# One decoder layer in float32 on one core: warm-up matmuls, an earlier first weight block, and first projection units that wait block by block

## The reference

```python
h = rmsnorm(x, attn_norm)
proj = h @ w_in            # columns: q, k, v of group A, q of group B, k and v of group B
out_a = dilated_attention(qa, ka, va, slopes_a)      # 16 heads
out_b = swa_sink_attention(qb, kb, vb, slopes_b, sinks)  # 16 query heads, 2 kv heads
mix = concat(rmsnorm(out_a, out_norm_a), rmsnorm(out_b, out_norm_b))
x = x + mix @ w_out
h = rmsnorm(x, ffn_norm)
x = x + (silu(h @ w_gate) * (h @ w_up)) @ w_down
return rmsnorm(x, final_norm)
```

## Time and profile before

| | |
|---|---|
| median of three runs | 2116.3 us |
| the profiled execution, device time | 2115.78 us |
| its span in the trace | 2114.0 us |
| TensorE matmul busy | 2055.0 us (97%) |
| VectorE busy | 1450.1 us (69%) |
| ScalarE busy | 874.0 us (41%) |
| DMA, mean over the span | 124 GB/s |
| mean granted TensorE clock | 0.992 of full speed |

### The profile page before, as it was taken

The page is one execution under the profiler, slowest core; times in us unless marked ns, Lnnn a source line. Parts: engine busy times, 40 slices in busy tenths (PEclk is TensorE's granted clock), DMA queues, the critical chain, the costliest instruction groups (busy, mean ns, idle before and its releaser), DMA issues.

```text
span 2114.0 us, 35232 instructions
## 1 busy us (share of the span) xinstructions
PE 2055.0 (97%) x12886; PEld 1857.5 (88%) x12886; DVE 1450.1 (69%) x2175; ACT 874.0 (41%) x1380; POOL 119.4 (6%) x191
## 2 busy tenths in 40 slices
PE   8999999999999799999999999999997999999998
PEld 7888888887888699999999999999996888888887
DVE  5466666666665788787887878788785645555446
ACT  5355555554346433333333333333333333333333
POOL 0022222222100000000000000000000000000000
PEclk9999999999999899999999999999998999999999
DMA  6322222224233244344444444344446552534323
GB/s 184 90 73 72 74 75 75 70 74 150 84 112 129 85 141 134 122 137 124 130 129 131 130 121 140 121 130 135 126 130 234 204 175 99 174 123 150 135 99 129
DMA packets 315867, 261.62 MB, mean 124 GB/s; under 512 B 13872, under 2 KB 268128, under 8 KB 314720
## 3 DMA queue, kind: packets, MB, share of 16 engines
q1 hardware_dynamic: 308304, 248.11, 36.9%
q10 hardware_dynamic: 7440, 11.72, 1.6%
HBM read 228.31 MB, written 31.46 MB: 123 GB/s over the span
## 4 chain that ended last, share of the span: by engine, by line
PE 84%; issue 5%; DVE 5%; ACT 4%; DMA 1%; SPq 1%; ACTq 0%; DVEq 0%; POOLq 0%; POOL 0%
PE bank L426 18%; PE bank L428 18%; PE bank L427 18%; PE bank L467 9%; PE bank L468 9%; PE bank L469 9%; PE bank L554 1%; ACT probs L819 1%; ACT w_hi L776 1%; DMA raw<-in_w_down 1%; DVE w_lo L1164 1%; PE bank L571 1%; PE bank L570 1%; ACT qB_both L797 0%; DVE pt_lo L1173 0%
## 5 line engine op out<-in xcount | busy, mean ns | idle before, releaser
L426 PE MATMUL bank<-s_hi,t_hi 128*128 128x256 f32 x2464 | 700.5, 284 | 26.0 <-DVE t_lo L1445 14.7
L427 PE MATMUL bank<-s_lo,t_hi 128*128 128x256 f32 x2464 | 699.2, 284 | 0.0
L428 PE MATMUL bank<-s_hi,t_lo 128*128 128x256 f32 x2464 | 699.2, 284 | 0.0
L1164 DVE TENSOR_TENSOR w_lo<-raw,w_hi 128x512 fp32r<-128x512 f32 x364 | 253.0, 697 | 408.4 <-ACT w_hi L776 406.2
L996 ACT ACTIVATE t_hi<-t_raw 128x1792 fp32r<-128x1792 f32 x176 | 299.6, 1703 | 556.7 <-PE bank L428 539.7
L426 PEld LDWEIGHTS bank<-s_hi,t_hi 128*128 128x128 f32 x2464 | 475.2, 193 | 27.5 <-issue 26.6
L427 PEld LDWEIGHTS bank<-s_lo,t_hi 128*128 128x128 f32 x2464 | 475.1, 193 | 1.0 <-issue 1.0
L428 PEld LDWEIGHTS bank<-s_hi,t_lo 128*128 128x128 f32 x2464 | 475.0, 193 | 0.0
L1445 DVE TENSOR_TENSOR t_lo<-t_raw,t_hi 128x1792 fp32r<-128x1792 f32 x176 | 356.2, 2024 | 155.9 <-ACT t_hi L996 155.9
L776 ACT ACTIVATE w_hi<-raw 128x512 fp32r<-128x512 f32 x364 | 229.1, 631 | 514.3 <-PE bank L469 360.1
L467 PE MATMUL bank<-w_hi,down_hi 128*128 128x512 f32 x640 | 250.1, 391 | 14.3 <-DVE down_lo L1173 14.3
(11 more groups left out here) (162 smaller groups left out, 2283.2 us busy)
## 6 DMA issues: line engine op xcount, KB each, us to landing
raw<-in_w_down SPq DMA_DIRECT2D x176, 256.0 KB, 2.5
t_raw<-in_w_gate SPq DMA_DIRECT2D x174, 256.0 KB, 3.0
t_raw<-in_w_up SPq DMA_DIRECT2D x174, 256.0 KB, 3.4
raw<-in_w_in SPq DMA_DIRECT2D x136, 256.0 KB, 2.9
gu_mid<-gu_out SPq DMA_DIRECT2D x44, 512.0 KB, 3.8
gu_s<-gu_mid SPq DMA_DIRECT2D x44, 512.0 KB, 4.9
raw<-in_w_out SPq DMA_DIRECT2D x64, 256.0 KB, 2.5
x_first<-in_x SPq DMA_DIRECT2D x8, 512.0 KB, 7.7
```

Of the source, the lines that this page charges most:

```text
L426: nc.tensor.matmul(out_ap, st_hi, mv_hi, start=start, stop=False, skip_group_check=True)
L427: nc.tensor.matmul(out_ap, st_hi, mv_lo, start=False, stop=False, skip_group_check=True)
L428: return nc.tensor.matmul(out_ap, st_lo, mv_hi, start=False, stop=stop, skip_group_check=True)
L1164: nc.vector.tensor_tensor(w_lo[:, s, :], raw[:, s, :], w_hi[:, s, :].bitcast(F32), ALU.subtract).then_inc(w_lo_done, 1)
```

## The change

- SP loads w0 right behind x0 rather than behind x1, w1 behind x2, w2 behind x4, w3 behind x6. Each weight block is ahead of one x block that it stood behind.
- TensorE runs eight 128x128 float32 matmuls of `ones` against `ones` into bank 6, which nobody reads, before it waits for the identity and x0.
- The first four units become `first_unit(j)`: the wait for h_lo stands in front of each k, not in front of four, and the two turns of the next x block (`turn_two`) stand in the middle (after the second k) and at the end of units 0 to 2. Before unit 0 only k=0 to 3 are turned.
- ScalarE runs one tiny activation behind the wait for `ones`, which brings its table load forward.
- ScalarE and VectorE split w0 behind k=0 instead of behind k=3.

```diff
--- before.py
+++ after.py
@@ -25,6 +25,7 @@
 NC = D // SEQ
 PAIRS = HEADS // 2
 RING = 4
+WARM = 8
 AHEAD = RING - 1
 UNIT = 512
 WINDOW = 128
@@ -59,7 +60,7 @@
 BANK_X = (2, 3, 5, 7)
 BANK_SET = (BANK_G, BANK_X)
 
-START_SPLITS = ([(0, 0), (0, 1)], [(0, 2)], [(0, 3), (1, 0)], [(1, 1)])
+START_SPLITS = ([(0, 1)], [(0, 2)], [(0, 3), (1, 0)], [(1, 1)])
 FIRST_SQ = 4 * (NC - 1)
 
 LAST = [(t, n) for n in range(NC) for t in (0, 1)] + [(t, n) for t in (2, 3) for n in range(NC)]
@@ -318,7 +319,7 @@
         for n in range(2 * NC):
             cols = slice(256 * n, 256 * (n + 1))
             sp.dma_start(x_first[:, :, cols], x2[:, cols].rearrange("(t p) c -> p t c", p=P)).then_inc(x_loaded[n], 16)
-            if n % 2:
+            if n % 2 == 0:
                 load(0, n // 2, tall(w_in2, n // 2, 4 * D_A), first=True)
         for j in range(4):
             load(1, j, tall(w_in2, j, 4 * D_A + D_KV))
@@ -669,27 +670,37 @@
                         n = KD + 2 * PAIRS
                         nc.tensor.transpose(bank[BANK_PT][:, 0:n], gain_rows[0:n, P:2 * P], ident[0:n, 0:n]).then_inc(gains_turned, 1)
 
+        def turn_two(k0):
+
+            pe.wait_ge(x_loaded[k0 // 2], 16)
+            for k in (k0, k0 + 1):
+                turn_x(k)
+
+        def first_unit(j):
+
+            pe.wait_ge(w_lo_done, j + 1)
+            for k in range(4 * j, 4 * j + 4):
+                pe.wait_ge(xt_lo_done, k + 1)
+                ws = slice(P * (k % 4), P * (k % 4 + 1))
+                mm = three(bank[BANK_Q][:, :], w_hi[:, j, ws], w_lo[:, j, ws], h_hi[:, k, :], h_lo[:, k, :], k == 0, k == KD - 1)
+                if j < 3 and k % 2:
+                    turn_two(k + 3)
+            mm.then_inc(w_used, 1)
+
+        pe.wait_ge(ones_done, 1)
+        for i in range(WARM):
+            nc.tensor.matmul(bank[6][:, 0:P], ones[:, :], ones[:, :], start=True, stop=True)
         pe.wait_ge(ident_loaded, 16)
-
-        for k in range(8):
-            if k % 2 == 0:
-                pe.wait_ge(x_loaded[k // 2], 16)
-            turn_x(k)
-            if k == 1:
-
-                pe.wait_ge(gains_loaded, 16)
-                nc.tensor.transpose(bank[BANK_Q][:, 0:KD], gain_rows[0:KD, 0:P],
-                                    ident[0:KD, 0:KD]).then_inc(gains_turned, 1)
+        turn_two(0)
+        pe.wait_ge(gains_loaded, 16)
+        nc.tensor.transpose(bank[BANK_Q][:, 0:KD], gain_rows[0:KD, 0:P],
+                            ident[0:KD, 0:KD]).then_inc(gains_turned, 1)
+        turn_two(2)
         pe.wait_ge(gains_done, 1)
-        for s in range(8):
-            if s < 4:
-                pe.wait_ge(xt_lo_done, 4 * s + 4)
-            tall_unit(s // 4, s % 4, (BANK_Q, BANK_K)[s // 4], h_hi, h_lo)
-            if s < 2:
-                for k in range(8 + 4 * s, 12 + 4 * s):
-                    if k % 2 == 0:
-                        pe.wait_ge(x_loaded[k // 2], 16)
-                    turn_x(k)
+        for s in range(4):
+            first_unit(s)
+        for s in range(4, 8):
+            tall_unit(1, s % 4, BANK_K, h_hi, h_lo)
             if s == 6:
                 pe.wait_ge(xt_lo_done, KD)
                 spread_r(squares[:, :].rearrange("p (t c) -> p t c", c=P), 1, BANK_PT)
@@ -925,10 +936,14 @@
 
         act.dma_start(gain_rows[0:KD, 0:P], attn_norm[0, :].rearrange("(k p) -> k p", p=P)).then_inc(gains_loaded, 16)
 
+        act.wait_ge(ones_done, 1)
+        nc.scalar.activation(tick[:, 18:19], ones[:, 0:1], ACT.Copy)
         act.wait_ge(gains_done, 1)
         for n in range(NC):
             for k in range(4 * n, 4 * n + 4):
                 x_high(k)
+                if k == 0:
+                    split(0, 0, wait_slot=False)
             for u4, slot in START_SPLITS[n]:
                 split(u4, slot, wait_slot=u4 > 0)
             act.wait_ge(x_loaded[2 * n], 16)
@@ -1351,6 +1366,8 @@
         for n in range(NC):
             for k in range(4 * n, 4 * n + 4):
                 x_low(k)
+                if k == 0:
+                    split(0, 0)
             for u4, slot in START_SPLITS[n]:
                 split(u4, slot)
         for t in range(NT):
```

## The result

| | before | after |
|---|---|---|
| median of six runs | 2116.29 us | 2137.30 us |
| the profiled execution, device time | 2115.78 us | 2139.95 us |
| its span | 2114.0 us | 2138.2 us |
| mean granted TensorE clock | 0.992 | 0.983 |

The ratio is 1.0102, 95% interval 1.0088 to 1.0116. That is within 2%, but it is a real loss of 21 us, clear of the noise, and 20 us above the upper end of the predicted range (2117.2). The forecast was a gain of 1.5 us. One of the six runs before (7181 us) is an outlier; a median is not moved by it.

The account below looks back on a forecast made before the run. TensorE bounds the kernel; ScalarE's chain, set by w2's landing, decides when it enters the loops. The 1.5 us gain gave 2115.78 - 1.5 = 2114.3, or 2114.8 us against the median; range 2113.8 to 2117.2.

Parts of the forecast that it names:

- The step that failed: Whole kernel: the change acts only on the first 40 us, 2% of the span, so 42 us is out of reach.
- The warm-up's price: TensorE's start: eight matmuls end at 4.5 us, before x0 at 5.0; cost nothing, cover 0.5 us.
- Rival 2: TensorE's start: the clock falls in a new pause, losing 2.4 us, to 2117.2 us; chance 10%.
- The order of loads: Loads at the start: w2 lands at 15.1 instead of 16.67, so ScalarE's chain can start 1.55 us sooner.
- TensorE's stretch from x1 to k=7: TensorE's start: at fast pace `x_high` 7 is done at 15.2, a tie with w2's landing; gain 1.5 us.
- rival 1: TensorE from x1 on: clock at 1.2 GHz, 0.6 us slower than before, 2116.9 us; chance 25%.
- the landing of w2: ScalarE's start: w2's arrival, at 16.67 before and 15.1 forecast, sets ScalarE's chain.
- The units per k: First four units: waiting per k ends unit 3 at 26.6 instead of 30.2; TensorE gains 3.6 us, 1.5 stay.
- The wait before the spread: TensorE before the spread of the row norms: a new wait of about 2 us, spread starting at 37.1.
- The last 3.46 us, from the last square to the spread: End of the start: ScalarE's last square, VectorE's widening, then TensorE's spread; 3.46 us, untouched by the change.
- The table load: ScalarE's start: moves to an idle stretch with nothing on the chain; gives nothing.
- Rise of the clock: TensorE's start, kernel before: only transposes preceded the rise at 13.5 us, against the rule that transposes do not raise it.

Follow-up runs that it names:

- experiment 5: The kernel before with SP's new load order alone: 2115.39 us, ratio 1.0000.
- experiment 11: The whole change with TensorE's gate/up loop written out and the turns of x back in their old places: 2100.65 us, ratio 0.9937 to the kernel before.
- experiment 2: The changed kernel without the eight warm-up matmuls: 2114.96 us, ratio 1.0009 to the kernel before.
- experiment 12: The kernel before, loop kept, some third products left out so the gate/up body has 1797 instead of 2049 instructions (output differs): 2012.39 us, ratio 0.9513.
- experiment 3: The changed kernel with 48 redundant waits (24 more instructions) at TensorE's start: 2115.76 us, ratio 1.0010 to the kernel before.
- experiments 1 and 4: The kernel before with the eight warm-up matmuls alone: 2135.11 us; the kernel before with 64 redundant waits (32 instructions) alone: 2135.61 us.
- experiment 8: The kernel before with the warm-up matmuls, and 48 redundant waits in TensorE's stall ahead of the gate/up stage: 2114.37 us, ratio 0.9997.

## Why the prediction was wrong

**The step that failed** is the first: "Whatever the change does at the start therefore reaches the end only as an earlier or later moment at which TensorE enters the long loops". It also made the cap on the whole and left out the case that decided. The change reached the loops in a second way: TensorE's program is one row of instructions, and 32 more at the start move everything behind: the loop's target then stands 8 matmuls instead of 24 ahead of the next block that has to be fetched behind each jump back, which costs 2.0 us of standing still and some 2 us of slow clock a turn. The warm-up's price of "nothing, the cover 0.5 us" was right for the time in which they run (they ended at 4.77 us, x0's turns began at 5.10) and wrong for the kernel: +21 us. No rival had it. The trace did hold hints: the transfers of instruction blocks beside the pauses, the row "PE bank L426 <- issue: 10.3, 7, 1.8", and the pause in the earlier trace rows that I used for the clock alone. I took that pause as a constant of the kernel and never asked what it was released by, nor that six jumps had seven pauses, the seventh 24 matmuls behind a restart.

**A clock step I had about the right size for, at the wrong place.** Rival 2 priced a fall of the clock in a new pause at 2.4 us. It cost 1.2 to 2.5 us, but six times, in the loop. Of the two pauses that it named at the start (they measured 1.27 us at 22.15 and 1.73 us at 40.49) neither slowed a product.

**The order of loads: right.** W2's split at 15.2 was forecast and is 15.20 when the load order is changed alone (experiment 5); the spread follows by 1.4 us, where 1.5 was forecast.

**TensorE's stretch from x1 to k=7: rival 1 came true** (it had 25%). The clock fell at 9.61 us, 0.4 us into x1's turns and behind the 2.32 us wait for x1, rose again at 13.02, and the six products of k=0 and 1 came at 0.42 us. `X_high` 7 ended at 17.25 where that rival had 17.3, and w2's split at 17.14 where it had 17.3. So the landing of w2 set nothing any more.

**The units per k: mis-sized, with the wrong sign.** I counted what a wait per k gives VectorE's last h_lo, and not what six products (1.4 us) between two turns take from ScalarE, which needs both turns. Once per unit: 0.90 us of ScalarE's waiting at 15.98 and again at 26.51. The twelve products of unit 3 ran from 26.66 to 29.5 us, where the forecast had 26.6 for their end, and experiment 11 gives some 3 us back. The wait before the spread was forecast at 2 us and is 1.73; it only stands later.

**The last 3.46 us, from the last square to the spread**, are 3.45 (37.04 to 40.49): untouched, as said. **The table load**: nothing, as said.

**Rise of the clock.** Warm-up matmuls do quicken what follows: x0's and x1's turns take 1.59 us for eight, where they took 1.94 and 1.97. The views give 1.00 where a trace has no record of the clock. The first record, of 1.00, is at 6.20 us after and at 13.39 before, where the pace rises too; so in the kernel before the rise did come behind transposes alone. But from 9.61 us on the pace is half again, so the warm-up matmuls give 0.7 us here (experiment 2 against the change, the spread at 41.23 and 40.49).

## What to carry to other kernels

An instruction added ahead of a loop on the same engine moves the loop in the program, and behind a jump back that can cost more than the instruction: here 32 instructions cost 21 us whether they were matmuls or redundant waits, and 24 further ones gave it back. So when an edit's effect is too large, or shows in a stage that it doesn't touch, look at the "issue" waits behind the loop's restart, and try the same kernel with a few redundant waits ahead of the loop before explaining the edit; look when the instruction blocks land, and where a loop with a long body shows such pauses, write it out. Between two turns that one `x_high` pair needs, put no products.

## What was not expected of the hardware

- A jump back over a body of 1797 or 2049 instructions makes TensorE stand still for 1.4 to 2.3 us, some 2.0 us from start to start; over one of 639 or 827 nothing that the trace shows. Long bodies are brought again at every turn, in blocks of 16,384 bytes; short ones are not.
- TensorE goes on 1.6 to 1.9 us after the block that a jump back needs has landed, and 1.2 to 1.6 us after the block behind it.
- A second pause follows where a fixed border in the program lies 8 or 16 matmuls behind the target: 2.0 us and 1.1 us on average. It ends 2.8 to 4.2 us, mostly some 3.3, behind the restart.
- Pauses this short can bring the clock from 1.00 to 0.50, for 3.4 or 6.8 us, and their length alone doesn't decide it. In experiment 12 it fell behind three single pauses of 1.8 to 1.9 us (0.9 to 1.3 us behind the restart) and not behind three others of 1.7 to 2.1 us; in experiment 3 single pauses of 2.2 and 2.3 us left it up. Two pauses of 1.4 to 2.7 us with eight matmuls between them brought it down at all 18 jumps (after, experiments 1 and 4).
- Instructions that do nothing are not free where an engine is late: in experiment 3 the 48 redundant waits at the very start made the warm-up begin at 3.6 us, and x0's turns at 7.1 (the spread came no later for it, at 40.47 us against 40.49); moved into a stall (experiment 8) they delay nothing there.
